# Feed-forward blocks of a ten-sublayer float32 network: one 512-column matmul for the high weight halves, and the down projection in two passes

## What is computed

```python
def rms_norm(x, g, eps=1e-6):
    xf = x.astype(jnp.float32)
    y = xf * lax.rsqrt(jnp.mean(xf * xf, axis=-1, keepdims=True) + eps)
    return (y * g.astype(jnp.float32)).astype(x.dtype)

def swiglu_ffn(x, w_in, w_out):            # 1024 -> 2 * 2816 -> 1024
    gate, up = jnp.split(x @ w_in, 2, axis=-1)
    return (jax.nn.silu(gate) * up) @ w_out

x = x + 0.5 * swiglu_ffn(rms_norm(x, norm_ffn1[l]), ffn1_w_in[l], ffn1_w_out[l])
```

## Time and profile before

| | us |
|---|---|
| median of 3 runs | 1751.66 (1747.46 to 1752.46) |
| the profiled execution's own time | 1749.16 |
| its span (first to last instruction) | 1747.4 |
| PE busy | 1653.9 (95%) |
| DVE busy | 1036.4 (59%) |
| POOL busy | 848.5 (49%) |
| ACT busy | 630.4 (36%) |

### The profile page before, as it was taken

The page is one execution under the profiler, slowest core; times in us unless marked ns, Lnnn a source line. Parts: engine busy times, 40 slices in busy tenths (PEclk is TensorE's granted clock), DMA queues, the critical chain, the costliest instruction groups (busy, mean ns, idle before and its releaser), DMA issues.

```text
span 1747.4 us, 30862 instructions
## 1 busy us (share of the span) xinstructions
PE 1653.9 (95%) x12070; PEld 1559.8 (89%) x12070; DVE 1036.4 (59%) x1455; ACT 630.4 (36%) x826; POOL 848.5 (49%) x1064
## 2 busy tenths in 40 slices
PE   6999999958899999999999999999999997799999
PEld 6999988738789999999998899997799996589999
DVE  5655555986356556865565575553665546447555
ACT  5434321020054335433325444333444333344342
POOL 5866200200079775787500397640686720059772
PEclk9999999968699999999999999999999998799999
DMA  6655333200156554465534466543565532056552
GB/s 252 216 181 182 119 133 108 85 1 1 46 173 216 181 181 156 145 205 181 180 109 157 157 204 194 180 157 121 193 202 184 181 108 97 13 170 216 182 186 77
DMA packets 72240, 263.42 MB, mean 151 GB/s; under 512 B 8016, under 2 KB 8144, under 8 KB 72016
## 3 DMA queue, kind: packets, MB, share of 16 engines
q1 hardware_dynamic: 72144, 262.08, 44.8%
HBM read 261.00 MB, written 1.05 MB: 150 GB/s over the span
## 4 chain that ended last, share of the span: by engine, by line
PE 86%; DVE 9%; ACT 2%; DMA 1%; issue 1%; POOL 1%; SPq 0%; DVEq 0%; ACTq 0%
PE ps L1331 14%; PE ps L1332 14%; PE ps L1333 14%; PE ps L1347 10%; PE ps L1377 7%; PE ps L1379 7%; PE ps L1378 7%; PE ps L1389 4%; PE ps L1400 2%; DMA raw<-blocks 1%; POOL w_lo L421 1%; DVE arena L1277 1%; PE ps L1689 1%; PE ps L1460 1%; DVE xn_lo L750 1%
## 5 line engine op out<-in xcount | busy, mean ns | idle before, releaser
L421 POOL TENSOR_TENSOR w_lo<-raw,w_hi 128x256 fp32r<-128x256 f32 x1048 | 836.4, 831 | 735.0 <-ACT w_hi L477 731.3
L1331 PE MATMUL ps<-xn_hi,w_hi 128*128 128x256 f32 x2112 | 604.6, 286 | 29.2 <-DVE xn_lo L750 24.7
L477 ACT ACTIVATE w_hi<-raw 128x1024 fp32r<-128x1024 f32 x396 | 416.4, 1059 | 594.1 <-PE ps L1333 379.4
L1332 PE MATMUL ps<-xn_lo,w_hi 128*128 128x256 f32 x2112 | 601.1, 285 | 0.0
L1333 PE MATMUL ps<-xn_hi,w_lo 128*128 128x256 f32 x2112 | 601.0, 285 | 0.0
L1331 PEld LDWEIGHTS ps<-xn_hi,w_hi 128*128 128x128 f32 x2112 | 408.8, 194 | 33.3 <-DVE xn_lo L750 14.7
L1332 PEld LDWEIGHTS ps<-xn_lo,w_hi 128*128 128x128 f32 x2112 | 409.0, 194 | 0.4 <-issue 0.2
L1333 PEld LDWEIGHTS ps<-xn_hi,w_lo 128*128 128x128 f32 x2112 | 409.0, 194 | 0.0
L1377 PE MATMUL ps<-h_hi,w_hi 128*128 128x256 f32 x1056 | 299.1, 283 | 0.0
L1378 PE MATMUL ps<-h_lo,w_hi 128*128 128x256 f32 x1056 | 298.8, 283 | 0.0
L1379 PE MATMUL ps<-h_hi,w_lo 128*128 128x256 f32 x1056 | 298.8, 283 | 0.0
(11 more groups left out here) (275 smaller groups left out, 1256.8 us busy)
## 6 DMA issues: line engine op xcount, KB each, us to landing
raw<-blocks SPq DMA_DIRECT2D x491, 512.0 KB, 3.3
cst<-consts SPq DMA_DIRECT2D x1, 2358.0 KB, 14.9
x<-x_in SPq DMA_DIRECT2D x4, 256.0 KB, 7.1
out<-x SPq DMA_DIRECT2D x4, 256.0 KB, 2.6
cst<-consts SPq DMA_DIRECT2D x1, 109.0 KB, 2.0
```

The source lines that it names most:

```text
L421: ins = nc.gpsimd.tensor_tensor(w_lo[:, slot(n), piece], raw[:, slot(n), piece], w_hi[:, slot(n), piece], ALU.subtract)
L477: nc.scalar.activation(w_hi[:, slot(n), :], raw[:, slot(n), :], ACT.Copy)\
L1331: nc.tensor.matmul(where, wh, xn_hi[:, k, :], start=k == 0 and opens, stop=False)
L1332: nc.tensor.matmul(where, wh, xn_lo[:, k, :], start=False, stop=False)
```

## The change

1. **One matmul for two products.** The activations' halves lie side by side (`xn[:, k, 0:2, :]`, `hid[:, c, 0:2, :]`). `w_hi` is multiplied with both in one matmul of 512 columns into a whole PSUM bank, and `w_lo` with the high half in a second one of 256 columns. The bank's right half then holds the w_hi·x_lo part, which someone has to add.
2. **PSUM.** A gate or up tile takes a whole bank, so only two tiles c are in flight (banks 4, 5 and 6, 7), and `gate_up(c)` waits for `halves_added` of tile c - 2. Eight output tiles would need eight banks, so the down products run in two passes: *near* (output tiles 0 to 3, in banks 0 to 3, in step with the hidden tiles) and *far* (tiles 4, 5 in banks 4, 5, then 6, 7 in banks 0, 1), after the last hidden tile. All hidden tiles are kept in `hid`. Near blocks are 512 columns wide; a far block has 256 columns of four down blocks (of two in the short ones), 12 per feed-forward, fetched in rows of 1 KB.
3. **The two halves of gate and up.** ACT copies the right halves out of PSUM (`low_part`, 512 elements), DVE adds the left halves (512), and multiplies both by `rstd` in one operation (512). ACT takes Silu instead of Sigmoid, and one DVE multiplication goes.
4. **Who splits.** DVE takes the up blocks of the odd tiles from 5 on (`up_on_vector`) besides the near blocks, and it does them inside `hidden(c)`, between the multiplication by `rstd` and the wait for Silu. POOL has the rest.
5. **The end.** The far blocks are split by POOL and DVE in turn; x gets its pairs 0 and 1 before the far pass ends, each by two additions. The loops are written out.

```diff
+def up_on_vector(c):
+    return c > LEAD and c % 2 == 1
...
             def ffn(f, n0):
-                def step(k, i=0):
-                    for n in range(n0 + down_block(k) + 6, n0 + down_block(k) + 9):
-                        if n < end and is_split(n):
-                            hi(n, 2 * i)
-                    sigmoid(k + LEAD, i)
+                def silu(c):
+                    tile_up, b = n0 + gate_block(c) + 1, 4 + 2 * (c % 2)
+                    act.wait_ge(used[slot(tile_up)], nth(tile_up))
+                    nc.scalar.activation(low_part[:, :, :], ps[:, b:b + 2, SEQ:], ACT.Copy).then_inc(low_taken, 1)
+                    act.wait_ge(gate_ready, NFC * f + c + 1)
+                    nc.scalar.activation(gs, gate_up[:, 0, :], ACT.Silu).then_inc(gs_ready, 1)
...
+                for c in range(LEAD, NFC):
+                    hi_until(n0 + stored_down(c - LEAD) + 8)
+                    silu(c)
...
-                def hidden(c, i=0):
+                def hidden(c, between=None):
+                    b = 4 + 2 * (c % 2)
+                    v.wait_ge(low_taken, NFC * f + c + 1)
+                    nc.vector.tensor_tensor(gate_up[:, :, :], ps[:, b:b + 2, 0:SEQ], low_part[:, :, :], ALU.add)\
+                        .then_inc(halves_added, 1)
+                    v.wait_ge(halves_added, NFC * f + c + 1)
+                    nc.vector.tensor_tensor(gate_up[:, :, :], gate_up[:, :, :], over(rstd[:, :], 2), ALU.mult)\
                         .then_inc(gate_ready, 1)
...
+                    if between:
+                        between()
+                    v.wait_ge(gs_ready, NFC * f + c + 1)
...
+                def weights(c):
+                    lo(n0 + near_block(c - 1))
+                    if c == NFC - 1:
+                        lo(n0 + near_block(NFC - 1))
+                    elif up_on_vector(c + 1):
+                        lo(n0 + gate_block(c + 1) + 1)
...
+            def three_products(where, hi, lo, both, opens, closes):
+                high = both[:, 0, :]
+                if not closes:
+                    nc.tensor.matmul(where, hi, both.rearrange("p a t -> p (a t)"), start=opens, stop=False)
+                ins = nc.tensor.matmul(where[:, 0:SEQ], lo, high, start=False, stop=False)
...
-                for k in FIRST_STEPS:
-                    step(k)
...
+                for k in range(FFN_STEPS):
+                    down(k)
+                    gate_up(k + LEAD)
+                down(NFC - 3)
+                down(NFC - 2)
+                far_products(n0, 0)
+                down(NFC - 1)
+                for i in range(1, N_FAR):
```

More of the change, by code:

```diff
@@ L139, in slot, with nth, columns_of, nth_split @@
     return n % RING
-def nth(n, i=0):
-    return n // RING + 1 + i
+def nth(n):
+    return n // RING + 1
 def is_split(n):
[L149 to L157, removed]
+    return KINDS[n] in ("gate", "up", "near", "far", "far_short")
+def columns_of(n):
+    return HALF if KINDS[n] in ("near", "far_short") else BLK
+SPLITS_SO_FAR = [sum(is_split(m) for m in range(n % RING, n + 1, RING)) for n in range(NRING)]
+def nth_split(n):
+    return SPLITS_SO_FAR[n]
+def up_on_vector(c):
+    return c > LEAD and c % 2 == 1
+def far_on_vector(i):
+    return i > 0 and i % 2 == 0
 class Chain:
     def __init__(self, engine, sem):
-        self.engine, self.sem, self.count, self.later = engine, sem, 0, 0
+        self.engine, self.sem, self.count = engine, sem, 0
     def __call__(self, ins):
@@ L457, in _ @@
                             lo(n)
-                    for k in FIRST_STEPS:
-                        step(k)
[L460 to L464, removed]
+                    for c in range(LEAD, NFC):
+                        lo(n0 + gate_block(c))
+                        if not up_on_vector(c):
+                            lo(n0 + gate_block(c) + 1)
+                    for i in range(N_FAR):
+                        if not far_on_vector(i):
+                            lo(n0 + far_block(i))
         @block.scalar
@@ L488, in preload, with norm @@
                 chain(nc.scalar.activation(table[:, 0:4], table[:, 4:8], func))
-            def norm(version, gains, then=ACT.Sigmoid):
+            def norm(version, gains, then=ACT.Silu, after=None):
                 for a in range(4):
+                    if after:
+                        hi_until(FIRST[after] + (far_block(4), far_block(6), far_block(11), FFN_BLOCKS + 4)[a])
                     if version:
@@ L1318, in _, with feature_tiles @@
             pe.wait_ge(gains_loaded, 16)
-            def feature_tiles(tiles, i=0, after_norm=None, between=None):
+            def three_products(where, hi, lo, both, opens, closes):
[3 more added lines that the diff above has]
+                ins = nc.tensor.matmul(where[:, 0:SEQ], lo, high, start=False, stop=False)
+                if closes:
+                    ins = nc.tensor.matmul(where, hi, both.rearrange("p a t -> p (a t)"), start=False, stop=True)
+                return ins
+            def feature_tiles(tiles, after_norm=None, between=None):
                 for k in range(KD):
```

404 lines of the change are left out of this document (212 added, 192 removed).

## The result

The changed kernel takes **1922.4 us** (median of 4 runs, 1921.66 to 1924.76), the kernel before 1749.6 beside it: a ratio of **1.099 (95% interval 1.098 to 1.1005)**. It is slower by 10%, as the forecast of 1912 us (1785 to 1970) had it. The profiled execution took 1921.66 us with a span of 1919.8.

The account below looks back on a forecast made before the run. The prediction took the spacing of PE's matmuls as the bound. Its terms, -76.0 + 144.2 + 18 + 20 - 2.9 + 0.7 + 43 + 16 = +163, on 1749 gave 1912 us, 8-in-10 range 1785 to 1970.

Parts of the forecast that it names:

- part 1: PE's matmul groups: merging takes a group of three from 0.360 to 0.336 us, -76.0 us over 3168 groups.
- part 2: Steady steps: PE waits 2.67 us for DVE's up-block `w_lo` in every second step, 54 times, +144.2 us.
- part 3: Feed-forward starts: `gate_up(2)` waits for tile 0's halves, a 3.4 us pause, net six times 3.0, +18 us.
- part 4: Last tiles: PE waits for near block 20's `w_lo` from DVE, six times 3.3, +20 us (16 to 23).
- part 5: Seams between feed-forwards: earlier pairs of x remove PE waits, -2.9 us; last addition as two operations, +0.7 us.
- part 6: TensorE clock: 3.4 us at 1.2 GHz follow every second of 54 pauses, +43 us, and 10 of 12 longer ones, +16.
- The clock stays up: Rival: pauses as forecast, but TensorE's clock does not fall behind them; 1853 us, chance 22%.
- DVE isn't slowed by POOL: Rival: the chain to `w_lo` takes 5.3 us, pauses of 1.27 us, no clock loss; 1774 us, chance 12%.
- Cost by columns: Rival: a matmul's cost goes with its columns, a group stays 0.360 us, merging gains nothing; 1970 us, chance 12%.
- Faster: Rival: the chain to `w_lo` is 4.03 us or less, so PE does not wait mid feed-forward; 1709 us, chance 7%.

Follow-up runs that it names:

- experiments 5 and 6: Second: changed kernel with DVE's low halves and ACT's copy moved ahead, starts reordered too, 1721.3 us; first: that kernel with each merged matmul split in two, 1746.5 us.
- experiment 9: Separate kernel without the computation, only matmul streams of known widths: 0.1200 us for 256 columns, 0.2270 for 512, 0.353 per alternating pair.
- experiment 1: Changed kernel with the low half of DVE's up block made before DVE waits for the tile's sums: 1754.1 us, ratio 1.0044.
- experiments 2 and 3: First: changed kernel with ACT's copy ahead of the high half, 1807.8 us; second: changed kernel with nine zero matmuls ahead of each of 54 pauses, 1883.7 us.
- experiment 4: Changed kernel with each merged 512-column matmul taken apart into two of 256 columns: 1923.5 us, ratio 1.101.
- experiment 8: Changed kernel with GpSimd computing only 32 of 1,024 columns of its low halves past the first twelve blocks: 1817.0 us, ratio 1.039.

## Why the prediction was right, and where its sizes were off

The forecast hit the direction and the mechanism of its largest term. That it hit the time within 10 us is luck in part: the merged matmul brought 51 us less than forecast, and pauses, starts, last tiles and clock together cost 44 us less.

| term | forecast | measured | from |
|---|---|---|---|
| part 1, merged matmul | -76.0 | -25 | experiments 5 and 6; 9 |
| part 2, 54 pauses | +144 | +115 | trace, 54 x 2.13 (mean, less the 0.23 of the matmul before) |
| part 3, starts | +18 | +13 | trace, 17.9 us of pauses against 5.0 before |
| part 4, last tiles | +20 | +17 | trace, six waits, start to start less 0.12 |
| part 5, seams | -2 | -2 | waits for `xn`, 22.5 us against 24.7; the addition not separated |
| part 6, clock | +59 | +52 | 115 us more at 1.2 GHz x 0.45 |
| sum | +163 | +170 | the time itself: 172.5 (1921.66 - 1749.16) |

**Part 1 failed in its size.** The step was "I take 0.216 us, because the longer float32 matmuls show next to nothing above their stream". Those rows are of another kind of matmul: in the changed kernel's own stream the 512-column one stands 0.231 us before its follower, and alone it takes 0.227. The 0.012 us that the prediction itself found above the stream for 256 columns is a cost for each matmul and doesn't vanish with width; the nearer row was that one. Merging takes away one such cost in three, 0.0133 us, and alternating widths give back 0.005 of it (0.3516 against 0.347): 0.008 where 0.024 was taken. The Trainium skill's rule ("TensorE: Matmul & The Clock Gate", section "Back-to-back issue gap") gives N/2.4 + 2.5 ns for an isolated warm matmul, which the prediction left unsaid; by it the gain would have been 8 us in all. The measured 25 us lies between it and the forecast, with the slope as the rule has it and a constant of 13.3 ns. For a stream with weight loads, as this one is, the same section of the Trainium skill gives some 131 ns at 512 columns, and the 0.2270 us of experiment 9 contradicts that.

**Part 2 was right in mechanism and 0.6 us long.** Of the 0.63 us between 2.67 and 2.04, 0.19 are the groups (12 of them fill 4.22 us instead of 4.03) and 0.44 the chain. In the chain the multiply was taken at 1.21 us, beside GpSimd, and took 0.68 to the next start, though GpSimd was at work; near and up together took 2.82 to the next start where 1.21 + 1.65 was said, the copy 0.58 to 0.69 as bounded. So the slowing is real, but not each operation gets it in full: the multiply's mean is 0.817, between the two rows. The bounds of 1.27 to 2.77 us held it. The condition under which the prediction called itself wrong altogether, the split of up block c+1 done before PE is through gate block c+1, is just what experiment 1 makes true.

**Parts 3 and 4** came out in kind, and somewhat smaller. Three of the six starts pause 3.41 us from start to start, 3.18 without the matmul before (3.4 predicted); the others have 6.66, 1.65 and 0.77 us, which the one-start sum didn't foresee. Nor did it see that the kernel before already paused 3.78 us from start to start at the start of the third feed-forward, where the 6.66 now stand. At the last tiles a wait is 2.8 us on the mean (3.3 predicted). At the start of the fourth feed-forward, four high halves stand ahead of the copy, as said:

```profile
1083.88 3.47 ACT L530 ACTIVATE w_hi<-raw 128x1024 fp32r<-128x1024 f32 x4
1087.26 0.57 ACT L591 ACTIVATE low_part<-ps 128x512 f32<-128x512 f32 x1
...
1088.61 0.50 PE L1404 MATMUL ps<-xn,w_hi 128*128 128x512 f32 x1 [3.02 <-DVE arena L866]
```

The far loads, for which there was no row, land in time, even at more than the whole blocks' 3.3 us of before; the page of the changed kernel has

```profile
raw<-blocks SPq DMA_DIRECT2D x419, 512.0 KB, 4.1
raw<-blocks SPq DMA_DIRECT2D x144, 256.0 KB, 3.9
```

and PE names no DMA among its long waits.

**Part 6 was a guess between two rows, and its size came out, though not for its reason.** The prediction argued that pauses of 2.67 us lie just above the 2.4 that was followed by 1.2 GHz, and that the 2.3 was not the earlier trace rows. The real pauses are shorter than both: the clock fell behind about every second one of 1.88 us idle in the profile, where the pause of the earlier trace rows that was not followed by 1.2 GHz had 2.05 us idle (2.43 from start to start). The kernel before also has one of the same length, 2.44 us from start to start, ending at 494.08 us, that was followed by 3.4 us at 1.2 GHz. So length alone does not decide, and that the clock term came out is luck. Its parts also differ: some 102 us at 1.2 GHz behind the 54 pauses cost 46 us (43 said), and all the rest 6 (16 said). That the pauses bring the clock down was argued then and is shown now, by experiments 2 and 3. Longer pauses do it more often: 2.05 us of standing still in the changed kernel, 1.95 in experiment 4 and 0.98 in experiment 2 gave 232, 198 and 136 us at 1.2 GHz in the whole trace, where the kernel before has 117.

**The rivals.** "The clock stays up" (1853) is refuted by the 0.940. "DVE isn't slowed by POOL" (1774) falls with experiment 8; its price was also too low, as the run without the slowing is at 1817, mainly since the merged matmul brings 51 us less than its sum had. "Cost by columns" (1970) was wrong in its reason, but its price for the merged matmul, no gain, was only 25 us from the truth, the forecast's 51. "Faster" was priced at 1709 with a chain short enough; the best version, which is that case with the ends mended as well, is at 1721.

What stays open: why the starts differ among each other, why one pause is followed by 1.2 GHz and the next like it is not, and what makes a pair of alternating widths 0.005 to 0.006 us dearer than the two alone.

## What to carry to other kernels

When a change shortens the bounding engine's work, ask which engine hands it its next operand, and write out that engine's program in order: here one subtraction, ready to be done, stood behind a wait for a result that it didn't need, and that cost 168 us where the merged matmul brought 25. A producer should do what is ready before it waits for what isn't. And the value of an edit on a waiting engine can't be read from the time: taken apart under the pauses, the merged matmul was worth nothing, and without them 25 us.

## What the runs showed of the hardware that was not expected

- An fp32r matmul costs its columns at 2.4 GHz plus 0.0133 us at 256 as at 512 columns (0.1200 and 0.2270 us), while the records of plain float32 ones lie 0.216 and 0.429 us apart, next to nothing above two streams of their columns. A plain float32 matmul leaves two such records (48 matmuls, 96 records in experiment 9). 448 columns stand out by 0.007 us (0.2067).
- Adding 486 matmuls of zeros made the kernel 39 us faster, by keeping TensorE at 2.4 GHz through its waits. Standing still for 2.05 us every 17 us brought it to 1.2 GHz behind about every second pause, 0.98 us every 15 us never mid feed-forward.
- Beside GpSimd, a DVE subtraction of two SBUF operands is a third slower (1.64 against 1.225 us at 1,024 elements, 0.935 against 0.689 at 512), an addition with one operand in PSUM not at all (0.691 in both).
